# Turning keys and values of the gated scan with whole transposes

## What is computed

```python
k = (1.0 - lb_d) * jax.nn.sigmoid(-z)               # keys; logf is the log of the gate, q the asks, i the values
def step(S, inp):                                    # one chunk of tokens, S is [64 keys, 64 values]
    g = jnp.cumsum(lf_c, axis=2)
    inter = jnp.einsum('bhtk,bhkv->bhtv', q_c * jnp.exp(g), S)
    scores = jnp.einsum('bhtk,bhsk,bhtsk->bhts', q_c, k_c, rel)
    o = inter + jnp.einsum('bhts,bhsv->bhtv', scores, i_c)
    S = jnp.exp(g_last)[..., None] * S + jnp.einsum('bhsk,bhsv->bhkv', k_c * jnp.exp(g_last - g), i_c)
```

## Time and profile before

| | |
|---|---|
| median of 3 runs | 5550.07 us (5545.63 to 5558.74) |
| the profiled execution: its time | 5547.89 us |
| its span | 5546.1 us |
| TensorE busy (matmul) | 4903.5 us, 88% |
| VectorE busy | 3398.0 us, 61% |
| ScalarE busy | 1866.0 us, 34% |
| mean granted clock of TensorE, share of full speed | 0.946 |

### The profile page before, as it was taken

The page is one execution under the profiler, slowest core; times in us unless marked ns, Lnnn a source line. Parts: engine busy times, 40 slices in busy tenths (PEclk is TensorE's granted clock), DMA queues, the critical chain, the costliest instruction groups (busy, mean ns, idle before and its releaser), DMA issues. The chain is left out here.

```text
span 5546.1 us, 120203 instructions
## 1 busy us (share of the span) xinstructions
PE 4903.5 (88%) x51393; PEld 3755.2 (68%) x51393; DVE 3398.0 (61%) x5671; ACT 1866.0 (34%) x3105; POOL 1317.3 (24%) x1186
## 2 busy tenths in 40 slices
PE   5999999788887975979998679999897999979989
PEld 2788888677776863858886434444486888766767
DVE  5166566455557875867981678888654000258877
ACT  3244444233335432341111334444404000136642
POOL 4111111322320000350000047767535111000012
PEclk7999999899999987989999779999998999979999
DMA  8244344221211124643324310000364112220145
GB/s 291 84 140 165 140 144 144 93 72 59 69 58 67 51 71 170 209 127 97 113 94 158 114 46 18 24 18 14 108 194 128 70 67 75 98 96 34 41 130 159
DMA packets 446893, 561.50 MB, mean 101 GB/s; under 512 B 83022, under 2 KB 338010, under 8 KB 434346
## 3 DMA queue, kind: packets, MB, share of 16 engines
q1 hardware_dynamic: 376444, 366.28, 21.3%
q10 hardware_dynamic: 54622, 130.36, 6.1%
q0 software_dynamic: 15312, 57.45, 2.6%
HBM read 350.86 MB, written 203.12 MB: 100 GB/s over the span
## 5 line engine op out<-in xcount | busy, mean ns | idle before, releaser
L164 PE MATMUL p_bank<-p_hT_high,p_w_high 128*128 128x512 f32 (+1 forms) x2744 | 1037.7, 378 | 8.7 <-PEq L37 7.8
L166 PE MATMUL p_bank<-p_hT_high,p_w_low 128*128 128x512 f32 (+1 forms) x2744 | 1029.5, 375 | 0.0
L165 PE MATMUL p_bank<-p_hT_low,p_w_high 128*128 128x512 f32 (+1 forms) x2744 | 1029.4, 375 | 0.0
L164 PEld LDWEIGHTS p_bank<-p_hT_high,p_w_high 128*128 128x128 f32 x2744 | 517.4, 189 | 110.4 <-issue 17.5
L166 PEld LDWEIGHTS p_bank<-p_hT_high,p_w_low 128*128 128x128 f32 x2744 | 517.3, 189 | 93.9
L165 PEld LDWEIGHTS p_bank<-p_hT_low,p_w_high 128*128 128x128 f32 x2744 | 517.5, 189 | 91.6
L3011 POOL TENSOR_TENSOR at_acc<-at_acc,at_p 128x512 f32<-128x512 f32 x256 | 414.6, 1619 | 124.8 <-ACT at_p L2947 102.0
L2947 ACT ACTIVATE at_p<-at_sc 128x1024 f32<-128x1024 f32 (+1 forms) x296 | 284.7, 1013 | 378.9 <-PE at_sc L2838 373.0
L3053 DVE TENSOR_REDUCE at_mx<-at_mb 128x2 f32<-128x1024 f32 (+1 forms) x280 | 342.1, 1222 | 51.0 <-PE at_mb L2849 50.8
L164 PE MATMUL o_bank<-o_w_high,o_m_high 128*128 128x512 f32 x800 | 314.4, 393 | 64.6 <-POOL o_m_low L158 64.6
L1050 DVE COPY p_o<-p_bank 128x512 f32<-128x512 f32 (+1 forms) x52 | 33.8, 651 | 466.7 <-PE p_bank L166 466.7
(11 more groups left out here) (434 smaller groups left out, 9986.0 us busy)
## 6 DMA issues: line engine op xcount, KB each, us to landing
pT<-p_o ACTq DMA_DIRECT2D x128, 256.0 KB, 2.1
rwkv_chunks<-p_arr POOLq DMA_DIRECT2D x54, 512.0 KB, 5.3
o_z<-pT SPq DMA_DIRECT2D x50, 512.0 KB, 5.3
o_y<-y SPq DMA_DIRECT2D x50, 512.0 KB, 6.6
pT<-p_eo ACTq DMA_DIRECT2D x96, 256.0 KB, 2.0
rsc_X<-rwkv_chunks SPq DMA_DIRECT2D x54, 320.0 KB, 3.4
x<-o_o ACTq DMA_DIRECT2D x32, 512.0 KB, 2.7
o_x<-x SPq DMA_DIRECT2D x32, 512.0 KB, 4.6
```

What stands on the lines that cost most here:

```text
L164: nc.tensor.matmul(out, lhs[0], rhs[0], start=start, stop=False)
L165: nc.tensor.matmul(out, lhs[0], rhs[1], start=False, stop=False)
L166: return nc.tensor.matmul(out, lhs[1], rhs[0], start=False, stop=stop)
```

## The change

`turn` had six products with the identity: two for the keys, each of 64 tokens by 128 channels into its half of the partitions, and four for the values, each half chunk into both halves. It now has two transposes of 128 by 128, one for the keys and one for the values, 256 columns of `tb` in place of 384. `turned` copied `tb` to `KI` in one copy of 384 columns. It now makes the doubled values with four copies: for each a, one of 64 partitions and 2 x 128 columns (keys and values of half chunk a, on their own partitions), and one of 64 partitions and 128 columns (the values of half chunk a, to the other half of the partitions). What `KI` holds is the same.

```diff
@@ turned(g), on ScalarE
                     act.wait_ge(t_prod, g + 1)
-                    nc.scalar.copy(KI[g % NK][:].rearrange("p a t -> p (a t)"), tb[g % 2][:, 0:3 * P]).then_inc(t_evac, 1)
+                    ki, made = KI[g % NK], tb[g % 2][:, 0:2 * P].rearrange("p (a t) -> p a t", a=2)
+                    for a in range(2):
+                        ra, rb = slice(a * HD, (a + 1) * HD), slice((1 - a) * HD, (2 - a) * HD)
+                        nc.scalar.copy(ki[ra, 0:2 + a:1 + a, :], made[ra, :, :])
+                        last = nc.scalar.copy(ki[rb, 1 + a, :], made[ra, 1, :])
+                    last.then_inc(t_evac, 1)
@@ turn(g), on TensorE
                     if g >= 2:
                         pe.wait_ge(t_evac, g - 1)
-                    for a in range(2):
-                        chunk, ra = slice(c * P + a * HD, c * P + (a + 1) * HD), slice(a * HD, (a + 1) * HD)
-                        nc.tensor.matmul(tb[g % 2][ra, 0:P], ke[p % 2][:, chunk], idn[:], start=True, stop=True)
-                    for a in range(2):
-                        chunk = slice(c * P + a * HD, c * P + (a + 1) * HD)
-                        for x in range(2):
-                            last = nc.tensor.matmul(tb[g % 2][x * HD:(x + 1) * HD, (1 + a) * P:(2 + a) * P], v[m % 2][:, chunk], idn[:], start=True, stop=True)
-                    last.then_inc(t_prod, 1)
+                    nc.tensor.transpose(tb[g % 2][:, 0:P], ke[p % 2][:, c * P:(c + 1) * P], idn[:])
+                    nc.tensor.transpose(tb[g % 2][:, P:2 * P], v[m % 2][:, c * P:(c + 1) * P], idn[:]).then_inc(t_prod, 1)
```

## The result

The changed kernel took 5561.83 us (median of 19 runs, 5553.79 to 5572.44), the kernel before 5546.34 (19 runs, 5536.36 to 5558.74): a ratio of 1.0028, interval 1.0022 to 1.0035, about 15.5 us more. The forecast was 5548 and no change. The profiled execution's span is 5557.3 us against 5546.1, with a mean granted clock of 0.943 against 0.946, and its 11.2 us are all in the gated scan: from the first `front` to the last it takes 341.6 us instead of 330.2. What follows stage by stage is read from these two executions, and so adds up to about 11 us and not to 15.5.

What follows compares the result with a forecast made beforehand. In the gated scan it saw TensorE and VectorE close together at the top, VectorE unbroken in long stretches. Delay +5.9, recovery -4.9 and phase 5 -2.6 made -1.6 us: 5548 us, about no change, range 5536 to 5562.

Steps and rivals of the forecast that it cites:

- the 0.50 us a set: ScalarE in the gated scan: four overlapping copies take 0.86 us against 0.36 for one, 0.50 more a unit.
- The bound without overlap: Upper bound for ScalarE's four copies if none overlap: 0.92 us more a unit.
- the slower rival: Rival that ScalarE becomes the bound, its copies not overlapping or half partitions costing more; +15.8 us, 5566; chance 0.12.
- 5.9 were forecast: Delay from extra copies where ScalarE makes the next phase's sigmoids, phases 0 to 4: 1.5, 1.2, 1.0, 1.2, 1.0 us.
- the signs named as proof against it: Phase 0 over 2 us shorter; set over 1.1 us; stage clock below 0.94; phases 1 and 3 changing over 2 us.
- the recovery: Ends of phases 0 to 4: faster TensorE closes VectorE's holes, so 4.9 of the 5.9 us come back.
- a rival by itself (0.04): Gated scan: fewer TensorE records and longer waits bring more lower-clock time; +11 us needs some 22 us more; chance 0.04.
- TensorE's turn: Turning in the gated scan: 0.42 us replaces 0.71, saving 0.29 a unit with a back; turn to back 0.37.
- 2.6 in phase 5: Phase 5, where TensorE is nearly full: about nine units at 0.29 us saved, 2.6 us.
- ScalarE becomes the bound: Copies without overlap or dearer half partitions, 0.92 us each in 20 sets, nothing recovered: +15.8 us, 5566; chance 0.12.
- the saving counts in half of the units: Rival: hidden slack in VectorE's unbroken stretches lets TensorE's 0.29 count; 50 units give 14.5 us, 5536; chance 0.12.

Runs made afterwards that it cites:

- the measured doses: Four kernels with two transposes, differing in ScalarE set length, against the kernel before: 0.36 us, -6.7 us; 0.78, +1.0; 1.31 (the change), +15.5; 1.64, +29.9.
- the transposes alone: Kernel before with the two transposes but its old single 384-column copy, last third of the tile left stale: 5542.93 us, ratio 0.9982.
- two copies a set: The changed kernel with only the two 64x256 copies from the sixth unit on, doubled values left stale: 5550.63 us, ratio 1.0001 to the kernel before.
- the copies alone: Kernel before with its six turning products, but four ScalarE copies of the change's shapes from the 384 columns: 5566.16 us, ratio 1.0033.

## Why the prediction was wrong

**The step that failed** is the 0.50 us a set, "since every row of neighbouring copies overlaps". It measured 0.95 before `keep`, 0.82 where `level` follows. The rows behind it were of copies over all 128 partitions; the change's copies alternate between halves, and no row that I used had that. The bound without overlap, 0.92 (its terms make 1.29 and so 0.93), was right to 0.03 us before `keep` and was given to the slower rival. In n 0 to 8 of phases 0 to 4 the scan grew by 10.6 us where 5.9 were forecast; 5.9 at 0.95 instead of 0.50 would be 11.2. By the measured doses a set of 0.86 us (0.08 above the 0.78) would have given about 1.0 + 0.08 x 27 = 3.2 us (an estimate): no change by what can be measured here. So it is this term that makes a loss out of no change, and the sum was some 5 us too low even so. Three of the signs named as proof against it came: a set over 1.1 us, a scan whose clock is below 0.94, and phase 1 longer by 3.5 us (by the starts of `front`; phase 3 by 1.8).

**The second miss, the recovery.** 4.9 us were to come back at the phase ends, because TensorE paced them. With level copies at n 9 to 14 and a set of 1.31 us, ScalarE paces them at 2.65 us a unit where d = 0. From n 8 of phases 0 to 4 to the next phase the transposes alone win 4.1 us, and the change loses 1.6 (with phase 5, where nothing follows, 6.9 and 1.0 won). This second miss follows for the most part from the first: with two copies a set 3.1 came back there.

**The third, a wait that lengthens itself.** The clock was costed only as a rival by itself (0.04). In phase 0 it was a follow-up of ScalarE's delay, 1.47 of 3.84 us. The granted clock over the whole scan fell from 0.98 to 0.93, but the transposes alone have 0.94 and are faster, so a fall of that size can go with a gain. The rival asked for some 22 us more at the lower level if all were on the path; by the windows above the scan has about 35 more (0.07 x 341.6 / 0.5 less 0.02 x 330.2 / 0.5), the transposes alone about 25, and they are faster even so. How many of the 15.5 us it makes in all phases stays open: no kernel here held the clock and kept the waits.

**What held.** TensorE's turn: 0.37 us to `back`, and 0.05 on `back` itself (from its start to the next `front` 0.85 where it was 0.80): 0.29 saved, a dense unit at 2.42 instead of 2.71. Its worth: 2.6 in phase 5 and 4.9 at phase ends made 7.5 for the turn by itself, and the transposes alone gave 6.7. Phase 5 from n 8 on is 2.5 us shorter; but n 0 to 8 of it lost 1.8, which I had not counted, as that phase makes no gates for a next one. In n 3 to 8 of it the granted clock was 0.82 with the change and 1.00 before; with the copies alone it was 1.00, and the loss 0.7. So part of the 1.8 is likely the clock's, which was not shown by itself. VectorE's busy time is unchanged, 283.3 us over the scan.

**The rivals.** "ScalarE becomes the bound" came true with its place, its condition and the price of a set: no overlap, 0.92 each in 20 sets, nothing recovered, +15.8; measured +15.5. That the numbers agree so closely is in part luck: its 18.4 us for the 20 sets stand against 12.4 in n 0 to 8, its sum had no share of the clock, and none of the 1.8 us that phase 5 lost or of the 1.6 lost at the phase ends. Against "the saving counts in half of the units" stand the 6.7 us of the transposes alone, half of the 14.5 it asked for.

## What to carry to other kernels

When one instruction is split into several, price the neighbours' overlap by rows that have the same partitions, not by any neighbours; if there are none, take the bound without overlap as the likeliest. Work that is moved off the densest engine must be laid against the stretches where the receiving engine is full, not against its share of the stage (ScalarE was busy for half of this one, and most of the loss sits around stretches where it was at 90%). And before counting on a gain that comes back later, ask whether the engine just loaded becomes the pace there.

## What the runs showed of the hardware that was not expected

On ScalarE a copy started about 0.10 us before the one before it had ended only where its output began on the same partition as that one's, and its input too when both inputs lay in PSUM. The starts here are at partitions 0 and 64 alone. In the traces of the change and of the experiments the pairs with the same first partition at both ends, where the second had nothing to wait for, overlap (medians of 0.096 to 0.125 us, 19 to 216 pairs of a kind), and a pair in which the first partition of the output changes (0.011 to 0.024 after the end), or that of the input while both inputs lie in PSUM (0.012 after the end; 0.024 before `keep`), does not. Where the input goes from PSUM's upper half to SBUF's first partition and the output stays, as from the change's last copy to `level`'s, the overlap is there (0.097). In the copies alone, whose order has one pair with nothing changed, that pair overlaps, and so does `keep`: 1.08 us a set, 0.23 less than the change's.

```profile
1752.31 0.37 ACT L1971 COPY hg_KI<-hg_tb 64x256 f32<-64x256 f32 x1 [0.62 <-PE hg_tb L2173]
1752.69 0.26 ACT L1972 COPY hg_KI<-hg_tb 64x128 f32<-64x128 f32 x1
1752.85 0.37 ACT L1971 COPY hg_KI<-hg_tb 64x256 f32<-64x256 f32 x1
```

(ScalarE's timeline of the copies alone: 1752.31 + 0.37 ends before 1752.69, but 1752.69 + 0.26 ends after 1752.85.)

The Trainium skill, "VectorE: DVE Perf Modes", section Two Vector instructions with no wait between them, has a rule of this kind for VectorE: an instruction whose input from a memory, or whose output, starts in another group of 32 partitions than the last one there is held until the earlier ones have finished. ScalarE's pairs above, the one across two memories too, go by the same rule. The Trainium skill, "ScalarE: Activation LUTs", section What ACT_TABLE_LOAD costs, states an overlap of about 93 ns. That agrees with what the traces have for pairs on the same partitions, about 0.10 us; pairs on others do not have it.
